# Three small moves in the order of a mixer's work: a scaling on VectorE, a turn and a copy of rotated keys, two turns joined

## What is computed

```python
q = (rms_norm_2(q_lat, q_lat_norm) @ w_qb).reshape(b, s, 8, 64 + 32)      # "latent" queries
q_nope = rms_norm_2(q[..., :64], q_nope_gain)
q_rope = apply_rotary(rms_norm_2(q[..., 64:], q_rope_gain), cos, sin)
k_nope = rms_norm_2(kv[..., :64], k_nope_gain)
k_r = apply_rotary(rms_norm_2(k_rope, k_rope_gain), cos, sin)              # shared by the 8 heads
out_mla = blocked_causal_attention([q_nope, q_rope], [k_nope, k_r], v)
out_fox = blocked_causal_attention(rms_norm_2(fq), rms_norm_2(fk), fv, cumulative_log_forget)
mixed = sigmoid(g_mla + b0) * (out_mla @ w_branch_mla) + sigmoid(g_fox + b1) * (out_fox @ w_branch_fox)
```

## Time and profile before

| | |
|---|---|
| median of 3 runs | 1460.09 us |
| the profiled execution | 1459.98 us |
| its span, from the first to the last instruction | 1458.1 us |
| TensorE matmul busy (PE) | 1451.5 us, 100% |
| VectorE busy (DVE) | 1002.2 us, 69% |
| ScalarE busy (ACT) | 777.7 us, 53% |
| GpSimd busy (POOL) | 87.1 us, 6% |
| bytes by DMA | 266.82 MB, mean 183 GB/s |
| granted TensorE clock | 1.0 in all 40 slices |

### The profile page before, as it was taken

One profiled execution on the slowest core, in us unless ns is written; L12 is line 12 of the kernel. 1 busy time (PEld: TensorE's weight loads), 2 busy tenths in 40 slices (PEclk: granted clock), 3 DMA queues, 4 the chain that ended last, 5 costly groups with the idle time before them and its releaser, 6 DMA issues.

```text
span 1458.1 us, 18627 instructions
## 1 busy us (share of the span) xinstructions
PE 1451.5 (100%) x7822; PEld 1250.3 (86%) x7822; DVE 1002.2 (69%) x1216; ACT 777.7 (53%) x971; POOL 87.1 (6%) x113
## 2 busy tenths in 40 slices
PE   9999999999999999999999999999999999999999
PEld 7888888888888888888888888888888888888887
DVE  6876466777755877459877764787646987687753
ACT  6654355655534555345665544565436876465542
POOL 0000003000000000006100000000000800000000
PEclk9999999999999999999999999999999999999999
DMA  9855563556556555545465556465556543566552
GB/s 328 277 176 185 159 204 116 167 180 201 178 184 200 190 181 195 185 141 172 149 200 188 185 177 206 154 223 182 188 173 217 188 145 118 173 196 201 179 188 72
DMA packets 205620, 266.82 MB, mean 183 GB/s; under 512 B 6944, under 2 KB 148880, under 8 KB 205280
## 3 DMA queue, kind: packets, MB, share of 16 engines
q1 hardware_dynamic: 204320, 261.23, 54.7%
q0 software_dynamic: 1072, 4.35, 0.8%
q10 hardware_dynamic: 144, 0.05, 0.0%
HBM read 264.56 MB, written 1.05 MB: 182 GB/s over the span
## 4 chain that ended last, share of the span: by engine, by line
PE 93%; DVE 3%; ACT 1%; DMA 1%; issue 0%; SPq 0%; DVEq 0%; ACTq 0%
PE ps L631 31%; PE ps L638 17%; PE ps L563 14%; PE ps L565 13%; PE ps L564 13%; PE ps L616 1%; DMA raw<-in_ffn_wi 1%; DVE wlo L1656 1%; PE ps L741 1%; PE ps L836 1%; PE ps L774 1%; DVE d_i L2049 0%; ACT whi L1217 0%; DVE d_m L2045 0%; DVE d_i L2073 0%
## 5 line engine op out<-in xcount | busy, mean ns | idle before, releaser
L1656 DVE TENSOR_TENSOR wlo<-raw,whi 128x2048 fp32r<-128x2048 f32 (+5 forms) x275 | 567.3, 2068 | 259.1 <-ACT whi L1217 258.9
L1217 ACT CAST whi<-raw 128x2048 fp32r<-128x2048 f32 (+5 forms) x275 | 474.0, 1729 | 223.0 <-PE ps L565 218.5
L631 PE MATMUL ps<-xt,whi 128*128 128x512 f32 x2112 | 501.7, 391 | 0.8 <-DVE xt L2249 0.7
L631 PEld LDWEIGHTS ps<-xt,whi 128*128 128x128 f32 x2112 | 389.3, 188 | 78.0 <-DVE xt L2249 1.5
L638 PEld LDWEIGHTS ps<-xt,wlo 128*128 128x128 f32 x2112 | 267.1, 191 | 8.2
L638 PE MATMUL ps<-xt,wlo 128*128 128x256 f32 x2112 | 269.6, 283 | 0.0
L563 PE MATMUL ps<-whi,xt 128*128 128x512 f32 (+4 forms) x304 | 112.7, 371 | 0.0
L565 PE MATMUL ps<-whi,xt 128*128 128x512 f32 (+4 forms) x304 | 109.7, 361 | 0.0
L564 PE MATMUL ps<-wlo,xt 128*128 128x512 f32 (+4 forms) x304 | 109.5, 360 | 0.0
L563 PEld LDWEIGHTS ps<-whi,xt 128*128 128x128 f32 x304 | 57.3, 189 | 9.2 <-issue 1.0
L565 PEld LDWEIGHTS ps<-whi,xt 128*128 128x128 f32 x304 | 57.2, 188 | 8.5
(11 more groups left out here) (422 smaller groups left out, 1884.3 us busy)
## 6 DMA issues: line engine op xcount, KB each, us to landing
raw<-in_ffn_wi SPq DMA_DIRECT2D x85, 1024.0 KB, 5.0
raw<-in_ffn_wo SPq DMA_DIRECT2D x40, 1024.0 KB, 4.9
raw<-in_ffn_w_gate SPq DMA_DIRECT2D x22, 1024.0 KB, 5.1
raw<-in_ffn_w_up SPq DMA_DIRECT2D x22, 1024.0 KB, 5.1
raw<-in_ffn_w_down SPq DMA_DIRECT2D x20, 1024.0 KB, 4.9
raw<-in_w_in SPq DMA_DIRECT2D x14, 1024.0 KB, 5.1
raw<-in_even_w_in SPq DMA_DIRECT2D x6, 1024.0 KB, 5.2
raw<-in_ffn_wo SPq DMA_DIRECT2D x8, 512.0 KB, 3.8
```

The costliest lines, as they stand in the source:

```text
L631: return e.matmul(Pair(job.name).ap[:, b, :], whi[:, v % SPLIT, 256 * j + 128 * b:256 * j + 128 * b + 128], XS[:, j, :, :].rearrange("p h ...
L1217: e.copy(whi[0:n, v % SPLIT, c], raw[0:n, v % RAW, c]).then_inc(s_hi.mark(*[(v, j) for j in js]), 1)
L1656: e.tensor_tensor(wlo[0:n, v % SPLIT, c], raw[0:n, v % RAW, c], whi[0:n, v % SPLIT, c].bitcast(F32), ALU.subtract).then_inc(s_lo.mark(*[(v ...
```

## The change

The scaling of the latent queries on VectorE stands behind the normalised rows of the second fox group and one tile's subtraction, no longer ahead of a tile's subtraction and the first logits. The turn of the rotated keys on TensorE stands right behind the second fox values, no longer behind the first step of `gate2[2]`; the copy of those turned keys on ScalarE stands ahead of a tile's rounding, no longer behind it. The turn of the second fox group stands right behind that of the first, no longer after two steps of `gate2[0]`. Nothing is added or left out.

```diff
                 fox_turn(0)
-                steps(gate2[0], 0, 0, 2)
                 fox_turn(1)
-                steps(gate2[0], 0, 2, 3)
+                steps(gate2[0], 0, 0, 3)
                 fox_scores(0)
...
                 fox_values(1)
+                rope_key_turn()
                 steps(gate2[1], 1, 3)
                 give(gate2[1].name, s_dve["gate", 1])
                 steps(gate2[2], 0, 0, 1)
-                rope_key_turn()
                 mla_queries(0)
...
                 turned(("m_", "v", ("f", 1)), YT, 6, None, (128,) * 2)
-                unit()
                 q.wait_ge(*s_turn["m_", "s", ("f", 1), 0])
                 q.wait_ge(*s_turn["krt"])
                 e.copy(mKT[64:96, :, :], bc(Pair("krt").ap[64:96, 0, 0:256], 1, 8)).then_inc(s_act.mark("krt"), 1)
+                unit()
                 mla_queries(0)
...
                 head_factors("q")
                 unit()
-                head_scale("q")
                 unit()
                 logits(mat, ("f", 0), 0, causal)
...
                 normalise(mat, ("f", 1), 1)
                 unit()
+                head_scale("q")
                 head_sums("k")
                 head_factors("k")
```

## The result

The changed kernel takes 1462.53 us in the median of 22 runs (1461.63 to 1463.35) against 1460.00 us (1459.65 to 1460.32) for the kernel before, also in 22 runs: a ratio of 1.0017, 95% interval 1.0010 to 1.0023. That is 2.5 us slower. The interval leaves out 1, so the loss is real, but it is less than the 0.2% (2.9 us) that the prediction counts as no change, and the time lies inside the prediction's range.

A forecast was written before the change was run, and what follows sets the result against it. TensorE, busy 1451.5 of 1458.1 us, was taken to bound the kernel, with VectorE's slack of 0.80 us deciding. +1.45 at the latent queries' turn and -0.34 gave +1.1 on 1460.09: 1461.2 us, range 1459.0 to 1462.9.

The forecast's parts named there:

- VectorE's run: VectorE's gapless queue up to the subtraction for `gate2[2]`: without POOL's cost, 1.02 us late against a slack of 0.80.
- the forecast: POOL costs VectorE 0.7 to 2.2 us, so the kernel is +0.4 to +1.9 us slower; chance 0.60.
- the prediction's own signs: Right: keys' factors near 3.4 us, new TensorE wait about 1 us; wrong: factors 2.7 us, or waits over 3 us.
- the third rival: VectorE's SBUF instructions each wait out a whole POOL instruction: cost above 2.2 us, up to +5.0 us in total; chance 0.15.
- The first wait: TensorE ahead of the second fox scores, waiting for VectorE's logits: the wait goes, -0.86 us.
- The scaling: Four VectorE instructions on the latent queries, in their new place with POOL idle: 1.90 us.
- POOL's cost c: Cost to VectorE of POOL's rotation beside the keys' factors, keys' scaling and a subtraction: 1.45 us, bounded by 0 and 5.3.
- The fox values: TensorE at the second fox values: a new wait of over 1 us for VectorE's copy, not added to the later one.
- The second wait: TensorE ahead of the first latent scores, waiting for ScalarE's copy of the keys: the wait goes, -0.34 us.
- The joined turns: The two fox turns on TensorE, same transposes and matmuls in another order: 0 taken, at most 0.39 us of gain.
- The total: Latent queries' turn +1.45 us, then -0.34: +1.1 us on 1460.09, so 1461.2 us.

The follow-up runs named there:

- the part alone: Only the turn and copy of the rotated keys moved, against the kernel before: 1459.62 us, ratio 0.9997.
- one with a wait of 1.5 us: The changed kernel with POOL's rotation of the first token half replaced by one memset of a column: 1460.61 us, ratio 1.0005 to the kernel before.

## Why the prediction was right, and where its sizes were off

The time lies in the range and the place is right: VectorE's run without gaps, made longer by the scaling and by POOL's moved rotation, holds TensorE at the second fox values and `gate2[2]`. That the median stayed in the range is partly luck. It lies above the forecast's own +0.4 to +1.9 us, POOL's cost came out higher than forecast, and a second effect, the clock, was not in the sum at all. The slower of the two groups of executions, around 1463.0 us, is just above the range's upper end. By the prediction's own signs the trace lies between the forecast (factors near 3.4 us, a wait of about 1 us) and the third rival (a wait of over 3 us): 4.92 us and 2.6 us.

**The first wait** held: -0.86 was forecast, and the scores start at 1161.66, which is 1162.38 - 1161.66 + 0.15 = 0.87 us sooner, with no wait.

**The scaling** was put at 1.90 us and took 1.88. **VectorE's run** without POOL: with c at nothing the sum gives -0.34, and the kernel with the rotation left out lies 0.42 us under the one before.

**POOL's cost c** is the term that was mis-sized, in both halves. The prediction took 0.73 us for the factors, from the row of the fox keys, and 0.72 for the two scalings and the subtraction behind them. Measured: 2.25 us (4.92 - 2.67) for the factors and nothing for the rest, since POOL was done by 1187.29. The sum of 1.45 against 2.25 made it come out 0.8 us short. The row taken was too kind. POOL's instructions there worked on 16 x 256 elements with one input. Three of VectorE's instructions went through for each of POOL's, and only one in three was held, until 0.03 us behind POOL's end (1143.77 after 1143.12 + 0.62 = 1143.74). In the kernel before:

```profile
1143.51 0.26 DVE L1692 SCALAR_TENSOR_TENSOR ny<-nb,ny 128x16 f32<-128x16 f32 x1
1143.80 0.17 DVE L1688 TENSOR_TENSOR na<-ny 128x16 f32<-128x16 f32 x1
1143.84 0.61 POOL L2361 TENSOR_SCALAR m_kt<-m_c,m_fc 16x256 f32<-16x256 f32 x1
```

In the changed kernel, too, the held instructions end just behind POOL's, but they are held far longer: 0.43 us (0.60 against 0.17) beside the gain products and sums of 128 x 256, where two go through for each of POOL's, and 0.16 to 0.21 us beside the products of 128 x 128, where it is nearly one for one. So the instruction of 0.18 us that the prediction saw pass unhindered inside one of POOL's was no measure of the rotation. With 2.25, c lies at the lower edge of the third rival, which began at 2.2, and not in the forecast's own range of 0.7 to 2.2. For the factors that rival's mechanism, the two engines in turn, is nearer to what happened; its full price of 5.3 us did not come, since one or two VectorE instructions went through for each of POOL's and the scaling and subtraction behind the factors met no rotation.

**The fox values** were to wait over 1 us ahead of a later wait of the same kind. They wait 2.63 us, and the later one shrinks: the last matmul ahead of `gate2[2]` starts at 1190.83 and the first of it at 1191.36, 0.53 us for a step of 0.23, so 0.30 us. The direction of the account was right: what counts is the end of VectorE's run, 1189.02 + 2.29 = 1191.31, not the sum of the two waits.

**The second wait**: -0.34 forecast; 2.17 - 1.82 = 0.35 in the changed kernel, 0.35 in the part alone. **The joined turns**: 0 forecast and measured.

**The total**: the trace's own account gives 2.17 - 0.35 - 0.10 = +1.7 us for executions at full clock, against +1.1. What the prediction did not have at all is the clock. In the one profile that shows it, that of the scaling alone, it stands at half for some 3.4 us (worked out from the table by stretches: 0.8 + 2 + 0.6). About half of the changed kernel's executions show the lower mean clock and take 1.2 us more (1463.0 against 1461.8 in the middle of the two groups), and the median of all falls at the lower edge of these.

## What to carry to other kernels

When a step on VectorE is moved, see what its mark sets off on other queues: here the 1.9 us of scaling cost less than what it set off, nearly 7 us of GpSimd work that moved with it and came to lie on short VectorE instructions in a chain. Give the other engine only what it needs, early, and move the rest. And count a new wait of TensorE higher than its length, since the clock may fall in it: here a wait of 2.6 us cost another 1.2 us in about half of the executions.

## What the runs showed of the hardware that was not expected

A chain of 14 instructions, most of 0.17 us, became 1.8 times as long (4.92 against 2.67 us) beside POOL work that reads SBUF, while POOL lost only 0.12 us of 6.80. And a single idle stretch of TensorE of 2.6 us went with a lower granted clock in 12 of 22 executions; the same kernel with that stretch filled showed none in 11, and one with a wait of 1.5 us none in 10.
